# Layer 0's mixing in one block: projection, RWKV, attention and output projection interleaved in one order per engine

## The chip, the cores and the metric

One core of a Trainium2 chip runs the whole program. The metric is the time of one execution in microseconds (us) of device time. Engines are named as the profile names them: PE is TensorE's matmul side and PEld its weight loads, DVE is VectorE, ACT is ScalarE, POOL is GpSimd, SP is SyncE, which here issues all DMAs. All arithmetic is f32.

## The reference, cut to what matters

A decoder trunk of two layers over 256 tokens of width 1024. Each layer has a mixer with a residual add, then a mixture of experts with a residual add. Only layer 0's mixer is touched:

```python
u = rms_norm(h, norm_mix[0])
cols = u @ hyb_w_in[0]                          # 1024 -> 1696 RWKV + 1304 attention columns
y_rwkv = rwkv7_mix(cols[..., :RWKV_COLS], ...)  # 8 heads x 64; recurrence over tokens
y_nsa = nsa_mix(cols[..., RWKV_COLS:], ...)     # 8 query, 2 key heads; 3 branches
h = h + jnp.concatenate([y_rwkv, y_nsa], -1) @ hyb_w_out[0]
```

`rwkv7_mix` shifts its columns by one token, derives decay, gate and learning rate from three low-rank parts, and runs the recurrence `state = state*w + (state@a) b' + v k'`, `y = state@r` for each token, then a norm per head, a bonus term and the gate. `nsa_mix` adds three attentions, each times a gate of its own: over 15 compressed blocks (a two-layer network on 32 tokens each), over selected blocks (with 256 tokens all four blocks are selected, so it is causal attention with its own keys and values), and over a window of 512, again causal here.

## The kernel before, in words

Layer 0's mixer is four blocks, each of which all engines finish before the next begins.

`hyb_in` (lines 270 to 379): x is normed (`norm_act`, `norm_dve`), turned (`turn_pe`, `turn_act`) and projected. The weights come in seven groups of columns through a ring `wr` of three slots; a group's slot is loaded again when TensorE has finished the group three before it. The RWKV columns r, k, v come out channel-major, six jobs of 256 channels (`feat`), the low-rank parts in three small jobs (`lo`), the attention columns token-major in three groups (512, 512 and 280 columns). VectorE applies the token shift.

`rwkv` (from line 381): the recurrence in chunks of 64 tokens. There are 16 slots of 128 rows, each with two chunks of one head in its row halves. First, small products give decay, keys and their norm; then products of 64x64 (`nn`, `bar`, `kar`), masked by VectorE, and turnings (`bt`, `at`, `kt`, `vt`) prepare a triangular system per chunk. It is inverted in five levels (`LEVELS`, line 741 for all its products): in a level TensorE makes `prod` from the level's mask and the inverse so far, ScalarE copies it, TensorE makes two updates (`dT`, `dTT`) and VectorE adds them (line 522) and masks for the next level (line 505). Then come `wu`, the maps and states between chunks (`gains`, `queries`, `step`, `carried`), the part within chunks (`within`), and on VectorE the norm per head, bonus and gate.

`nsa` (from line 899): its weights are loaded, rotary positions applied, then q, keys and the compression's input are turned by head into 64 rows (line 1069). The compression is 64 accumulating matmuls of 64 rows (line 1084). Compressed scores, softmax, turning and output follow (lines 1103 to 1116), then eight units `UNITS` (half of the tokens, branch, key head): `scores` (line 1127; 128 keys for the first half of tokens, 256 for the second), mask and maximum on VectorE (lines 988 to 997), four exponentials on ScalarE (line 1048), turning (line 1139), copy (line 1055), output (line 1146), scaling and sum on VectorE. Unit i+1's scores stand ahead of unit i's turning in TensorE's queue.

`join_hyb` (the function `join`): both halves of `mix` are turned, the output weights loaded, and 32 matmuls (64 instructions, as each f32 matmul is two) give the residual's addend. The router and the experts of layer 0 follow in blocks of their own; their weights are loaded from the start of the router's block on.

The order on each engine is written out by hand in the block's functions, and waits are on per-engine counts: `at(mark)` names a finished operation. A PSUM bank is taken with `take`: the eight banks in turn, waiting for the read of the job that had the bank before.

Of the kernel before, what the change touches and what calls it, by code (L numbers as in the profile page):

```python
# [14 lines left out]
P = 128  # L15
# [56 lines left out]
FEAT, NFEAT = columns([("mu", 12), ("mu_w", 1), ("mu_a", 1), ("mu_g", 1), ("w0", 4), ("a0", 4), ("k_k", 4),  # L72
# [62 lines left out]
def build(nc, a, known, new):  # L135
# [101 lines left out]
    s_ld = {n: sem("ld_" + n) for n in ("small", "gain", "w0", "w1", "w2", "par", "out")}  # L237
# [11 lines left out]
    nsa = sb(hyb, "nsa", [P, HALVES, NSA_COLS])  # L249
    mix = sb(hyb, "mix", [P, HALVES, D])  # L250
    z = sb(hyb, "z", [P, 12, SEQ + 1])
    zlo = sb(hyb, "zlo", [P, 3, SEQ + 1])
    par = sb(hyb, "par", [P, 3 * RW + 2 * RW])
    proj = ExitStack()
    zz, lo3 = sb(hyb, "zz", [P, 12, SEQ]), sb(hyb, "lo3", [P, 3, SEQ])
    gain = sb(proj, "gain", [P, D])
    junk = sb(proj, "junk", [P, D])
    ss = sb(proj, "ss", [P, HALVES])
    rstd = sb(proj, "rstd", [P, HALVES])
    u = sb(proj, "u", [P, HALVES, D])  # L260
    uT = sb(proj, "uT", [P, KD, SEQ])
    wr = sb(proj, "wr", [P, 3, KD, BANK])

    GRP = [(0, 512), (512, 512), (1024, 512), (1536, 160), (1696, 512), (2208, 512), (2720, 280)]

    FJOBS = [(g, j) for g in range(3) for j in range(2)]
    LO = [(0, W_RANK), (W_RANK, A_RANK), (W_RANK + A_RANK, G_RANK)]
    w_hyb = a["hyb_w_in"][0].rearrange("(k p) n -> p k n", p=P)

    with nc.Block(name="hyb_in", no_gpsimd_drain=True) as block:  # L270

        @block.sync
        def _(sp):
            load(sp, "small", h[:, :, :], a["x"][0].rearrange("(t p) d -> p t d", p=P))
            load(sp, "small", cst[:, :], a["tables"])
            load(sp, "small", feat[:, :], a["feat"])
# [922 lines left out]
    hyb.close()  # L1199

# [841 lines left out]
```

## Time and profile before

| | us |
|---|---|
| median of 3 runs | 1801.09 (1800.7 to 1805.3) |
| the profiled execution | 1801.7 |
| its span | 1799.9 |
| TensorE busy | 1611.2 (90%) |
| VectorE, ScalarE busy | 425.4 and 270.6 |
| layer 0's mixer: projection; RWKV; attention; output projection | 0 to 109.8; to 208.3; to 345.9; to 384.9 |

How to read it: a busy TensorE is not TensorE at its peak. Its clock is granted at one of two levels, 2.4 GHz (shown as 1.00) or 1.2 GHz (0.50), and the same matmul lasts about twice as long at the lower one. Idle time of an engine costs nothing unless the work that sets the end waits for it.

### The profile page before, as it was taken

How to read it: one execution, taken by the hardware profiler on the slowest of the kernel's cores; microseconds unless marked ns; L12 is line 12 of the kernel's file. 1: busy time of each engine (PE TensorE's matmuls, PEld its weight loads, DVE VectorE, ACT ScalarE, POOL GpSimd, SP SyncE). 2: the span in 40 equal slices, each digit the busy share in tenths (PEclk: the TensorE clock that was granted, in tenths of full speed). 3: DMA queues.
4: the chain of work that ended last, by engine and by line, in shares of the span. 5: the costliest groups of instructions: out<-in, count | busy, mean ns of one | idle time of the engine just before them, and what ended most of it. 6: DMA issues, size and time to landing. Idle time of an engine off the chain costs nothing. (4 is left out here: it accounts for less than half of the span.)

```text
span 1799.9 us, 21666 instructions
## 1 busy us (share of the span) xinstructions
PE 1611.2 (90%) x8698; PEld 896.2 (50%) x8698; DVE 425.4 (24%) x1053; ACT 270.6 (15%) x525; POOL 8.3 (0%) x12
## 2 busy tenths in 40 slices
PE   6989588877999999999969998968699999999995
PEld 5658486643444343434448746734444434444442
DVE  1138614222111111111115305621311111111111
ACT  2032202221101010101010123211110111110011
POOL 0000000000000000000000001000000000000000
PEclk9979755578999999999979996579799999999998
DMA  6400200248999999999743410042899999999990
GB/s 219 138 1 3 50 0 1 94 162 332 411 411 404 413 405 409 413 404 411 316 153 141 144 71 1 0 187 77 341 415 407 411 404 412 404 412 403 412 393 36
DMA packets 86807, 459.93 MB, mean 256 GB/s; under 512 B 11072, under 2 KB 17344, under 8 KB 37344
## 3 DMA queue, kind: packets, MB, share of 16 engines
q1 hardware_dynamic: 86752, 459.15, 63.8%
q8 instruction: 40, 0.66, 0.2%
q14 instruction: 15, 0.12, 0.0%
HBM read 458.07 MB, written 1.05 MB: 255 GB/s over the span
## 5 line engine op out<-in xcount | busy, mean ns | idle before, releaser
L1513 PE MATMUL bank<-rawffn,xgffn 128*64 128x512 f32 x2048 | 451.9, 594 | 0.0
L1513 PEld LDWEIGHTS bank<-rawffn,xgffn 128*64 128x64 f32 x2048 | 144.2, 137 | 278.0 <-issue 274.1
L1553 PE MATMUL bank<-rawffn,aTffn 128*64 128x512 f32 x1024 | 233.8, 598 | 18.9 <-DVE aTffn L1461 18.9
L1461 DVE TENSOR_TENSOR aTffn<-bank,sgffn 128x256 f32<-128x256 f32 x64 | 27.2, 425 | 659.1 <-ACT sgffn L1433 659.1
L1483 PE MATMUL bank<-selffn,uxffn 128*128 128x128 f32 x1024 | 131.6, 283 | 10.4 <-DVE selwffn L1453 9.1
L1483 PEld LDWEIGHTS bank<-selffn,uxffn 128*128 128x128 f32 x1024 | 122.5, 196 | 35.5 <-issue 24.3
L1553 PEld LDWEIGHTS bank<-rawffn,aTffn 128*64 128x64 f32 x1024 | 67.8, 136 | 140.2 <-issue 109.7
L1522 PE MATMUL bank<-ysffn,selTffn 64*128 64x512 f32 x512 | 127.2, 615 | 1.6 <-DVE ysffn L1471 1.6
L1431 ACT COPY gusffn<-bank 128x512 f32<-128x512 f32 x64 | 37.5, 586 | 560.7 <-PE bank L1513 560.7
L1471 DVE COPY ysffn<-bank 128x512 f32<-128x512 f32 x64 | 44.3, 692 | 194.5 <-PE bank L1553 194.5
L1522 PEld LDWEIGHTS bank<-ysffn,selTffn 64*128 64x128 f32 x512 | 44.1, 186 | 83.8 <-issue 80.5
L1746 PE MATMUL bank<-uT,wr 128*128 128x256 f32 x384 | 85.1, 385 | 0.7 <-ACT uT L232 0.7
L1746 PEld LDWEIGHTS bank<-uT,wr 128*128 128x128 f32 x384 | 74.3, 194 | 11.5 <-ACT uT L232 1.1
L1423 ACT COPY xgffn<-bank 128x512 f32<-128x512 f32 x64 | 37.5, 586 | 225.4 <-PE bank L1483 225.4
L1754 PE MATMUL bank<-wr,uT 128*128 128x512 f32 (+1 forms) x160 | 58.7, 529 | 0.0
L1189 PE MATMUL bank<-wo_ssm,srcT_ssm 128*128 128x512 f32 x128 | 55.2, 593 | 2.5 <-DMA wo_ssm<-in_ssm_w_out 2.5
L1540 PEld LDWEIGHTS bank<-cst,gusffn 128*128 128x128 f32 x256 | 26.8, 141 | 50.1 <-issue 47.0
L362 PE MATMUL bank<-uT,wr 128*128 128x256 f32 x192 | 44.2, 395 | 0.7 <-ACT uT L232 0.7
L1540 PE MATMUL bank<-cst,gusffn 128*128 128x128 f32 x256 | 42.0, 287 | 1.4 <-ACT gusffn L1431 1.4
L1754 PEld LDWEIGHTS bank<-wr,uT 128*128 128x128 f32 x160 | 27.9, 190 | 30.2 <-issue 30.1
L1433 ACT ACTIVATE sgffn<-bank 128x256 f32<-128x256 f32 x64 | 24.6, 384 | 118.4 <-PE bank L1540 118.3
L362 PEld LDWEIGHTS bank<-uT,wr 128*128 128x128 f32 x192 | 38.2, 199 | 6.7 <-ACT uT L232 1.1
(357 smaller groups left out, 1384.5 us busy)
## 6 DMA issues: line engine op xcount, KB each, us to landing
rawffn<-in_moe_w_gate SPq DMA_DIRECT2D x128, 1024.0 KB, 6.7
rawffn<-in_moe_w_up SPq DMA_DIRECT2D x128, 1024.0 KB, 8.8
rawffn<-in_moe_w_down SPq DMA_DIRECT2D x128, 1024.0 KB, 7.4
wr<-in_ssm_w_in SPq DMA_DIRECT2D x10, 2048.0 KB, 9.0
wr<-in_hyb_w_in SPq DMA_DIRECT2D x5, 2048.0 KB, 13.1
wo_ssm<-in_ssm_w_out SPq DMA_DIRECT2D x4, 2048.0 KB, 16.4
wo_hyb<-in_hyb_w_out SPq DMA_DIRECT2D x2, 2048.0 KB, 10.4
cst<-in_tables SPq DMA_DIRECT2D x1, 1208.0 KB, 7.3
```

The lines of the kernel that those rows point to most:

```text
L362: i = nc.tensor.matmul(b[:, c * SEQ:(c + 1) * SEQ], wr[:, g % 3, k, (2 * j + c) * P:(2 * j + c + 1) * P], uT[:, k, :], start=(k == 0), sto ...
L1189: i = nc.tensor.matmul(bs[t][c][:, :], srcT[:, k, t * P:(t + 1) * P], wo[:, k // 4, k % 4, c * BANK:(c + 1) * BANK], start=(k == 0), stop= ...
L1423: nc.scalar.copy(xg[:, :, 4 * half:4 * half + 4, :].rearrange("p x k s -> p k x s"), bank[SIDE_BANK][:, :].rearrange("p (k x s) -> p k x s ...
L1431: nc.scalar.copy(gus[:, :, :], bank[GU_BANK][:, :].rearrange("p (q j) -> p j q", j=4)).then_inc(S["gus"], 1)
L1471: V.tensor_copy(ys[:, :], bank[Y_BANK][:, :]).then_inc(S["y"], 1)
L1483: i = T.matmul(bank[SIDE_BANK][:, k * P:(k + 1) * P].rearrange("p (x s) -> p x s", x=2), ux[:, t, 4 * half + k, :], sel[:, t, :, :], start ...
L1513: i = T.matmul(bank[GU_BANK][CAP * m:CAP * m + CAP, :], xg[:, odd, k, :], raw[:, slot, (k % 4) * FH:(k % 4 + 1) * FH], start=(k == 0), sto ...
L1522: i = T.matmul(bank[ACC[2 * t + n]][:, :], selT[CAP * n:CAP * n + CAP, x, t * P:(t + 1) * P], ys[CAP * n:CAP * n + CAP, :], start=start, s ...
L1540: i = T.transpose(bank[TURN_BANK][:, j * P:(j + 1) * P], gus[:, j, :], C("ident"))
L1553: i = T.matmul(bank[Y_BANK][CAP * n:CAP * n + CAP, :], aT[:, j, :], raw[:, slot, jj * D + n * BANK:jj * D + (n + 1) * BANK], start=(j == 0 ...
L1746: i = nc.tensor.matmul(b[:, c * SEQ:(c + 1) * SEQ], wr2[:, g % 3, k, (2 * j + c) * P:(2 * j + c + 1) * P], uT2[:, k, :], start=(k == 0), s ...
L1754: i = nc.tensor.matmul(b[:, 0:n], uT2[:, k, j * P:(j + 1) * P], wr2[:, g % 3, k, 0:n], start=(k == 0), stop=(k == KD - 1))
```

## The change

The four blocks become one, `hyb`, with one written order per engine. The columns of the input weights are reordered once on the host (attention first, then low-rank, k, r, v), in six groups; the ring has two slots. x is loaded first and ScalarE waits for it alone; the attention weights are loaded behind the first two groups. Attention's pieces stand between the channel-major projection jobs and then between the five levels; units 6 and 7 stand among the steps between chunks. The banks are two pools of four: `left` for projection, attention and join, `right` for RWKV. Head pairs share one 128-row tile: q, keys and the compression's input are turned 128 columns at a time, keys doubled into both row halves, and scores, compressed scores and compression are pairs of 64-row matmuls in rows 0 to 63 and 64 to 127 that go to two banks. Decay and learning-rate columns are one low-rank job. The output projection adds the attention half first, then the RWKV half by halves of tokens; its weights are loaded during the levels and steps. Many tiles now share memory (`front`, `wr`, `z`, `qk`, `zz`), and several VectorE operations no longer wait for the one before.

`by_tokens(g, n)` is the old token-major group (2x8 matmuls of n columns), `by_channels` half of an old channel-major group (16 matmuls of 256 columns), `weights_turned` and `attended` the turning and the output product of a unit, `products` and `grown` the two halves of a level; `masked`, `grown`, `maps`, `carried` and `output` on VectorE hold the operations of before.

```diff
-    turn = {"n": 0, "at": {}, "last": [None] * 8}
-
-    def take(pe, *job):
-
-        b = turn["n"] % 8
-        turn["n"] += 1
+    turn = {"n": {}, "at": {}, "last": [None] * 8}
+
+    def take(pe, *job, pool=tuple(range(8))):
+
+        n = turn["n"].get(pool, 0)
+        turn["n"][pool] = n + 1
+        b = pool[n % len(pool)]
...
@@ the sync queue of the new block
+            load(sp, "x", h[:, :, :], a["x"][0].rearrange("(t p) d -> p t d", p=P))
+            load(sp, "gain", gain, row_src("mix0"))
             load(sp, "small", cst[:, :], a["tables"])
             load(sp, "small", feat[:, :], a["feat"])
-            load(sp, "gain", gain[:, :], row_src("mix0"))
-            for g, (c0, n) in enumerate(GRP):
-                if g >= 3:
-                    sp.wait_ge(*at("group", g - 3))
-                load(sp, f"w{g % 3}", wr[:, g % 3, :, 0:n], w_hyb[:, :, c0:c0 + n])
+            for g in range(2):
+                load(sp, f"w{g}", wr[:, g, :, 0:GRP[g][1]], w_hyb[:, :, GRP[g][0]:GRP[g][0] + GRP[g][1]])
             load(sp, "par", par[0:W_RANK, 0:RW], a["rwkv_w_up"][0])
-            load(sp, "par", par[0:A_RANK, RW:2 * RW], a["rwkv_a_up"][0])
-            load(sp, "par", par[0:G_RANK, 2 * RW:3 * RW], a["rwkv_g_up"][0])
-            load(sp, "par", par[:, 3 * RW:4 * RW], row_src("gn_w"))
-            load(sp, "par", par[:, 4 * RW:5 * RW], row_src("gn_b"))
+            load(sp, "par", par[W_RANK:W_RANK + A_RANK, 0:RW], a["rwkv_a_up"][0])
+            load(sp, "par", par[0:G_RANK, RW:2 * RW], a["rwkv_g_up"][0])
+            load(sp, "par", gn_w, row_src("gn_w"))
+            load(sp, "par", gn_b, row_src("gn_b"))
+            for x, n in enumerate("kv"):
+                load(sp, "nsaw", w2[:, x, :], a["nsa_w2_" + n][0])
+                load(sp, "nsaw", pe_[HD * x:HD * x + HD, :], a["pe_" + n])
+            sp.wait_ge(*at("turn", "mix0", 1, 1))
+            for x, n in enumerate("kv"):
+                load(sp, "nsaw", w1[HD * x:HD * x + HD, :, :], a["nsa_w1_" + n][0].rearrange("(l d) m -> d l m", d=HD))
+            for g in range(2, 6):
+                sp.wait_ge(*at("group", g - 2))
+                load(sp, f"w{g % 2}", wr[:, g % 2, :, 0:GRP[g][1]], w_hyb[:, :, GRP[g][0]:GRP[g][0] + GRP[g][1]])
+            sp.wait_ge(*at("vt", 1))
+            sp.wait_ge(*at("bt", 1))
+            load(sp, "w2", zz[:, :, :].rearrange("p (k c) t -> p k (c t)", k=3), wv_hyb[:, 4:7, :])
+            load(sp, "w2", wo_n[3], wv_hyb[:, 7, :])
+            sp.wait_ge(*at("wu", 1, 1))
+            for k in range(4):
+                load(sp, "wj", wo_r[k], wv_hyb[:, k, :])
...
@@ vector: levels and attention, then the steps
+            scores(2)
+            masked(1)
+            compressed_turned(0)
+            output(1)
+            grown(1)
+
+            scores(3)
+            masked(2)
+            dve.wait_ge(*at("read", "bon"))
+            dve.wait_ge(*at("read", "vt", 1))
+            go(V.tensor_tensor(heads_(pre), heads_(vt), rep(bon[:, :, :].rearrange("p t n -> p (t n)"), HD, 2),
+                               ALU.mult))
+            output(2)
+            compressed_out(0)
+            grown(2)
...
+            scores(7)
+            output(6)
...
+            maps(1)
+            maps(2)
+            maps(3)
+            carried(1)
+            output(7)
+            carried(2)
...
@@ scalar: the same stretch
+            weights_read(1)
+            products_read(1)
+            by_token("vt", vt, 0)
+            by_token("vt", vt, 1)
+            exps(2)
+            weights_read(2)
+            products_read(2)
+            exps(3)
+            by_token("kt", kt, 0)
+            by_token("kt", kt, 1)
+            weights_read(3)
+            products_read(3)
+            exps(4)
...
@@ tensor: projections with pieces between
+            by_tokens(0, 512)
+            new[("group", 0)] = ("pe", PE.n)
+            by_tokens(1, 512)
+            new[("group", 1)] = ("pe", PE.n)
+            by_tokens(2, VG)
...
+            by_channels(3, NK, 0)
+            pe.wait_ge(*at("blk", 1, 1))
+            bs = [take(pe, "hid", "mm", x, pool=left) for x in range(2)]
+            for l in range(CBLK):
+                for x in range(2):
+                    i = T.matmul(bs[x][:, 0:KV * NCMP], w1[HD * x:HD * x + HD, l, :], blk[HD * x:HD * x + HD, l, :],
+                                 start=(l == 0), stop=(l == CBLK - 1))
+                    if l == CBLK - 1:
+                        i.then_inc(pe_done, PE.one(("hid", "mm", x)))
+            by_channels(3, NK, 1)
...
+                bs = [take(pe, "s", i, e, pool=left) for e in range(2)]
+                for m in range(2):
+                    for e in range(2):
+                        o = T.matmul(bs[e][:, m * w:(m + 1) * w], qT[at64(e), 2 * g + m, tok(t)],
+                                     kT[at64(e), br, g, 0:w], start=True, stop=True)
+                        if m:
+                            o.then_inc(pe_done, PE.one(("s", i, e)))
...
+            weights_turned(0)
+            by_channels(5, NV, 0)
+            attended(0)
+            scores(1)
...
@@ tensor: levels 1 and 2
+            weights_turned(1)
+            scores(2)
+            products(1)
+            pe.wait_ge(*at("zz", 11))
+            for t in range(HALVES):
+                turned(("vt", t), [v4[:, c, tok(t)] for c in range(4)], right)
+            compressed_turned(0)
+            attended(1)
+            grown(1)
+            weights_turned(2)
+            scores(3)
+            products(2)
+            compressed_out(0)
+            for t in range(HALVES):
+                turned(("kt", t), [kh[:, c, tok(t)] for c in range(4)], right)
+            attended(2)
+            grown(2)
...
@@ tensor: join
+            js = [[take(pe, "join", "hyb", t, c, pool=left) for c in range(2)] for t in range(HALVES)]
+            pe.wait_ge(*at("read", "turnn", 1))
+            pe.wait_ge(s_ld["w2"], 32)
+            for k in range(4):
+                for t in range(HALVES):
+                    for c in range(2):
+                        T.matmul(js[t][c][:, :], srcn[:, k, tok(t)], wo_n[k][:, c * BANK:(c + 1) * BANK],
+                                 start=(k == 0), stop=False)
+            pe.wait_ge(s_ld["wj"], 64)
+            for t in range(HALVES):
+                pe.wait_ge(*at("mixr", t))
+                turned(("turnr", t), [mixr[:, t, tok(c)] for c in range(4)], right)
+                pe.wait_ge(*at("read", "turnr", t))
+                for c in range(2):
+                    for k in range(4):
+                        i = T.matmul(js[t][c][:, :], srcr[:, k, tok(t)], wo_r[k][:, c * BANK:(c + 1) * BANK],
+                                     start=False, stop=(k == 3))
+                    i.then_inc(pe_done, PE.one(("join", "hyb", t, c)))
...
```

Levels 3 to 5 follow the same pattern: level l has `weights_turned(l)`, `scores(l+1)`, `products(l)`, `attended(l)`, `grown(l)`, and `compressed_turned(1)` with RWKV's `akv` in level 3, `compressed_out(1)` in level 5. Then `weights_turned(6)`, `scores(7)`, `wu`, `attended(6)`, `gains(0)`, `queries(1)`, `gains(1)`, `weights_turned(7)`, `gains(2)`, `queries(2)`, `queries(3)`, `attended(7)`, `within(0)`, the steps, and after the second step the turning of the attention half.

## Rows read from the trace of the kernel before

**Rows 1.** The page: busy time by engine; granted clock in 40 slices of 45 us

```profile
PE 1611.2 (90%) x8698; PEld 896.2 (50%) x8698; DVE 425.4 (24%) x1053; ACT 270.6 (15%) x525; POOL 8.3 (0%) x12
...
PEclk9979755578999999999979996579799999999998
```

**Rows 2.** Windows: length; busy PE, PEld, DVE, ACT, POOL (count); clock; DMA share, GB/s

```profile
0.00:19.19 19.19, 3.65 (x16) 3.27 (x17) 2.86 (x9) 7.70 (x12) 0.20 (x4) 1.00 0.92 339
19.19:63.30 44.11, 44.11 (x193) 38.18 (x193) 8.32 (x15) 2.94 (x5) 0.00 (x0) 1.00 0.35 124
63.30:73.80 10.50, 10.50 (x49) 6.12 (x49) 3.44 (x7) 1.31 (x3) 0.00 (x0) 1.00 0.55 200
73.80:109.80 36.00, 35.22 (x97) 18.07 (x96) 2.74 (x5) 1.93 (x4) 0.00 (x0) 1.00 0.18 56
109.80:150.20 40.40, 31.59 (x276) 22.82 (x276) 28.52 (x34) 19.41 (x32) 0.00 (x0) 0.66 0.01 1
150.20:180.50 30.30, 30.11 (x963) 30.02 (x963) 21.49 (x27) 7.66 (x14) 0.00 (x0) 0.94 0.02 4
180.50:195.90 15.40, 14.59 (x416) 14.31 (x416) 6.61 (x15) 4.37 (x7) 0.00 (x0) 1.00 0.02 4
195.90:208.30 12.40, 0.00 (x0) 0.00 (x0) 11.20 (x21) 0.60 (x2) 0.00 (x0) 0.60 0.00 0
208.30:252.40 44.10, 34.51 (x160) 32.69 (x160) 11.67 (x46) 7.28 (x17) 0.00 (x0) 0.54 0.28 50
252.40:286.00 33.60, 23.24 (x107) 20.50 (x108) 13.22 (x37) 3.25 (x11) 0.00 (x0) 0.50 0.00 0
286.00:345.90 59.90, 52.92 (x192) 43.55 (x192) 22.60 (x48) 19.70 (x68) 0.00 (x0) 0.50 0.00 1
345.90:353.70 7.80, 3.68 (x17) 3.34 (x17) 0.00 (x0) 2.35 (x4) 0.00 (x0) 0.50 0.86 327
353.70:384.90 31.20, 30.18 (x64) 12.96 (x64) 2.77 (x4) 0.00 (x0) 0.00 (x0) 0.92 0.13 53
400.00:900.00 500.00, 477.90 (x2454) 208.83 (x2456) 80.69 (x258) 51.41 (x102) 0.00 (x0) 0.98 0.96 394
```

**Rows 3.** Timeline: ScalarE's first read of x; DMA issues: the load of x

```profile
8.84 0.19 ACT L330 COPY junk<-h 128x1 f32<-128x1 f32 x1 [6.44 <-DMA feat<-in_feat]
...
h<-in_x SPq DMA_DIRECT2D x1, 1024.0 KB, 4.9
```

**Rows 4.** Groups by line and form, TensorE, attention block (208 to 346)

```profile
L1084 PE MATMUL bank<-blk,w 64*128 64x30 f32 x128 | 27.5, 396 | 5.0 <-DVE blk L936 5.0
L1146 PE MATMUL bank<-nsa,pT 128*128 128x64 f32 x96 | 22.6, 426 | 5.4 <-ACT pT L1055 5.4
L1127 PE MATMUL bank<-kT,qT 64*128 64x256 f32 x32 | 15.1, 651 | 0.0
L1139 PE MATMUL bank<-cst,pr 128*128 128x128 f32 x48 | 12.3, 428 | 1.5 <-ACT pr L1048 1.5
...
L1103 PE MATMUL bank<-kcT,qT 64*128 64x15 f32 x32 | 7.0, 371 | 0.3 <-DVE kcT L948 0.3
```

**Rows 5.** Timeline, 141.3 to 144.3: 64x64 products, then 128x128 turnings

```profile
141.37 1.92 PE L720 MATMUL bank<-ar,kh 64*64 64x128 f32 x64
...
143.21 0.86 PEld L678 LDWEIGHTS bank<-cst,bh 128*128 128x128 f32 x8 [0.17 <-issue]
143.22 1.09 PE L678 MATMUL bank<-cst,bh 128*128 128x128 f32 x8
```

**Rows 6.** Groups by form, TensorE, the levels (150.2 to 180.5)

```profile
L741 PE MATMUL bank<-triT,prod 64*64 64x64 f32 x320 | 10.9, 218 | 0.0
```

**Rows 7.** Groups by form, VectorE: levels (two rows), attention block (last row)

```profile
L522 DVE TENSOR_TENSOR triT<-bank,triT 128x512 f32<-128x512 f32 x10 | 6.9, 692 | 4.0 <-PE bank L741 3.5
...
L505 DVE TENSOR_TENSOR lv<-nrb,cst 128x1024 f32<-128x1024 f32 x4 | 4.9, 1222 | 0.1
...
L994 DVE SCALAR_TENSOR_TENSOR pr<-bank,cst 128x512 f32<-128x512 f32 x8 | 5.5, 692 | 8.5 <-PE bank L1127 8.5
```

More of the change, by code:

```diff
@@ new lines, in by_channels @@
+            def by_channels(g, kind, j):
+                w = weights(g)
+                b = take(pe, "feat", kind, j, pool=left)
+                for c in range(2):
+                    for k in range(KD):
+                        i = T.matmul(b[:, c * SEQ:(c + 1) * SEQ], w[:, k, (2 * j + c) * P:(2 * j + c + 1) * P],
+                                     uT[:, k, :], start=(k == 0), stop=(k == KD - 1))
+                i.then_inc(pe_done, PE.one(("feat", kind, j)))
+                if j:
+                    new[("group", g)] = ("pe", PE.n)
@@ new lines, in turned @@
+            def turned(job, cols, pool):
+                b = take(pe, *job, pool=pool)
+                for n, x in enumerate(cols):
+                    i = T.transpose(b[:, n * P:(n + 1) * P], x, ident)
+                i.then_inc(pe_done, PE.one(job))
+            pe.wait_ge(s_ld["small"], 32)
+            turn_pe(pe, "mix0", u, KD, ("u", "mix0"))
+            pe.wait_ge(*at("read", "turn", "mix0", 1, 1))
+            by_tokens(0, 512)
+            new[("group", 0)] = ("pe", PE.n)
+            by_tokens(1, 512)
@@ L652, in _ @@
             pe.wait_ge(*at("kk2"))
-            b = take(pe, "ksum")
+            b = take(pe, "ksum", pool=right)
             for c in range(4):
@@ new lines, in _ @@
+            pe.wait_ge(*at("read", "kT", 1))
+            scores(0)
+            pe.wait_ge(*at("read", "kcT"))
+            bs = [take(pe, "sc", e, pool=left) for e in range(2)]
+            for t in range(HALVES):
+                for m in range(4):
+                    for e in range(2):
+                        i = T.matmul(bs[e][:, (4 * t + m) * NCMP:(4 * t + m + 1) * NCMP], qT[at64(e), m, tok(t)],
+                                     kcT[at64(e), m // 2, :], start=True, stop=True)
+                        if t and m == 3:
+                            i.then_inc(pe_done, PE.one(("sc", e)))
@@ new lines, in _ @@
+            attended(2)
+            grown(2)
+            weights_turned(3)
+            scores(4)
+            products(3)
+            pe.wait_ge(*at("read", "vt", 1))
+            pe.wait_ge(*at("read", "kar", 1, 1))
+            for t in range(HALVES):
+                b = take(pe, "akv", t, pool=right)
+                for e in range(2):
+                    for c in range(4):
+                        for q in range(2):
+                            i = T.matmul(b[at64(q), (4 * e + c) * HD:(4 * e + c + 1) * HD],
+                                         akr[at64(q), slot(t, e, c), 0, :], vt[at64(q), t, head(e, c)],
+                                         start=True, stop=True)
+                i.then_inc(pe_done, PE.one(("akv", t)))
```

1103 lines of the change are left out of this document (548 added, 555 removed).

## The prediction

> **What bounds the kernel now.** I read the page first: TensorE is busy 90% of the span, but the row of its granted clock falls to 5 tenths in slices 6 to 8 [rows 1], which is 225 to 360 us. So a busy share says little there, and the second view is the table of windows, cut at the borders of layer 0's four blocks [rows 2]. Four things are to be seen in it. The projection (19.19 to 109.8) is TensorE back to back at clock 1.00. In the RWKV block, TensorE waits for VectorE ahead of the levels (28.5 us of VectorE in 40.4), runs back to back through them (30.1 of 30.3), and does nothing in the 12.4 us of the head norm. In the attention block (208.3 to 345.9, 137.6 us) TensorE is busy 110.7 us, nearly all at clock 0.50, and idle for 27. The output projection starts 7.8 us after its block, since turning its input and loading its weights lie there alone, and runs 30.2 us. After it the experts run with the DMA engines at share 0.96 (400 to 900): they start behind the block's end and their pace is the DMA's, so whatever layer 0 gains at 384.9 the span gains, one for one. The page's other slices belong to work that the change doesn't touch.
>
> **The change part by part.** All of layer 0's mixing up to the residual now is one block; I add up TensorE's queue in its new order, every piece at the full clock first, and correct for the clock at the end.
>
> *a. Start.* ScalarE's first read of x waited for three loads until 8.84; x alone landed 4.9 us after its issue at 0.74 [rows 3], thus 5.6. The chain behind it keeps its length: the first projection matmul at 19.19−3.2=16.0. The gain row now is the second load; the tables (wanted by TensorE 8 us later than before by ScalarE) hide behind the norm.
>
> *b. Token-major groups and low-rank columns.* The same 512+512+280 columns: 35.2 us [rows 2], by width 82 instructions of 512 columns at 0.43. The three low-rank jobs become two of equal length: 10.5×2/3=7.1. The first window of the projection holds 2.8 us of half clock (44.1 for six jobs of 32 instructions, half as wide and so 0.215 each, 6.9 a job); they stay: 45.1, to 61.1.
>
> *c. Channel-major jobs.* Six at 6.9: 41.4. The ring has two slots for three. A 2 MB load has at least the 13.7 us of a group to land, and takes 6.4 at the 327 GB/s of the join's load [rows 2]; I take no wait. If this cover is gone, 3 us for each of four loads.
>
> *d. Pieces between these jobs.* Attention's prices are those of before [rows 4] halved for the clock, where rows are pairs of 64-row halves halved again. The compression, 128 instructions in 27.5, becomes 13.7 and paired 6.9; the sixteen 128x128 turnings are 0.13 each at full clock [rows 5] against 0.256 at half. In this stretch: turning q and k 2.3, compression 6.9, its second layer 0.7, score units 0 and 1 1.0, compressed scores 1.8 (7.0 before), turned weights and output of unit 0 1.4: 14.1. RWKV's small products lie here too: the 31.6 us of TensorE ahead of the levels, at clock 0.66, are 21 at the full one, and half of them, 10.3, come before the last projection job. One wait stays, 1.5 us for the squared keys (VectorE's shift, then ScalarE) before the norm sum. Together 25.9.
> Does the pairing hold? No row has 64-row operands in both halves with 128 weight columns. The nearest is the level products, 64x64 on two diagonal quarters: 320 in 10.9 us, 34 ns each with the gaps [rows 6], against 214 ns for a 128-column instruction at half clock. I take the full halving; the other end is none, +6.9 for the compression, +5.8 for the scores, +1.8 for compressed scores: +14.
> The Trainium skill (TensorE: Matmul & The Clock Gate, Part 3: Packing small matmuls) says that a weight load runs beside matmuls in flight only where the row group differs, which is what the new row halves offer; by that rule the price is the paired one.
>
> *e. Ahead of the levels.* Here VectorE sets the pace as before, at 0.69 for a 512-wide operation and 1.2 for a 1024-wide one [rows 7]: after the last job come its copy and shift (2.3), four masks of the first product (2.5), three level operations (3.7) and, because the right-hand pool has four banks, four masks of the second product (2.5) among which the turnings wait for their banks: 11.0, and 0.7 for the last turning. 11.7. Sum so far: 61.1+41.4+25.9+11.7=140.1.
>
> *f. Levels.* TensorE's 30.3 us stay. Added: turnings of v and k 1.9, attention units 1 to 5 with the compressed turnings and outputs 18.0 (all 96 output instructions are 22.6 at half clock, 11.3 at full; all 48 turnings 12.3, thus 6.1; all 256-wide scores 15.1, thus 3.8), and 1.6 of handover. 51.8. VectorE in the same stretch has its 21.5 plus attention's 22: 44 of 52 us. It isn't the bound, but nearly: a late unit has 2x0.69 for scores [rows 7], 1.2 for the maximum (1024 wide, as the mask), 1.2 for the level mask, 1.2 for the gate pieces, 1.2 for output, then 4x0.69 for the sums of a level, 10 us against TensorE's 10.4. The first sum of a level is ready some 6.5 us after its start, VectorE comes to it at 8; the tail of the sums then falls behind the next turned weights and scores, which need no sum. So the level lasts 10 to 11 and not 5.7.
>
> *g. Inter-chunk steps.* 15.4 us, plus attention units 6 and 7 on TensorE 6.2, plus VectorE's output(6) ahead of the copies of the level result and output(7) between the two carried states, 3.4: 25.0.
>
> *h. Join.* The attention half of the output projection (32 instructions of 0.43) is 13.7 and covers the 12.4 us of the head norm; its weights were loaded long before. Then the RWKV half 13.7, two turnings with copy 2.6, the last add 1.0: 31.0. The 7.8 us of load and turning go.
>
> Sum: 16.0+45.1+41.4+25.9+11.7+51.8+25.0+31.0=247.9 against 384.9: 137.0 less. Semaphores, marks and table loads change at nothing: ScalarE has 79 us of work in 248 and its loads lie in waits.
>
> Two corrections. *Changing the tile shape*: when 64x64 products give way to 128x128 turnings, the products end at 143.29 by their row, the turnings' first instruction starts at 143.22 [rows 5], and the weight loads beside it stood 0.17 us; nothing bigger is seen. With some 45 such changes now (before about 10) this is between 0 and 8 us; I take 8, since each of them also ends a run of pairs. The Trainium skill (TensorEngine Tiling (Array Packing), Key Properties) says that a change of tiling mode drains the engine. That speaks against this interleaving; by the rule the 8 us are sure, and the trace agrees in size. *Clock*: attention alone never got out of 0.50 though TensorE was busy 88% of its last 60 us [rows 2]; the levels, at 0.94, did. Mixed about one to two, I expect the full clock for most of it, with stretches of half clock at the compression, behind the 3 us wait before the levels, and once or twice in them: 10 us. Ends: 0, and attention's whole 38 us again.
>
> 137−8−10=119. The profiled execution took 1801.7 (span 1799.9, so 1.8 lies around it), 0.6 over the median of the runs, 1801.09: 1801.7−119=1682.7, and I say 1682.
>
> **The rivals.**
> *R1, VectorE in order.* Scores, masks and outputs stand ahead of the level sums in one queue. If their waits (score product, turned weights, output product) fall in series and not beside TensorE's pieces, a level is TensorE's 10.4 plus VectorE's 9: 5x8.6=43 more, 1725. For it: VectorE waits for products at the sums of the levels already [rows 7] and 44 of 52 us leave little slack. Against: the order gives each of its operations a piece of TensorE's that doesn't need it.
> *R2, half clock through the levels.* The mixture counts as attention did. Then levels cost 30 more, attention 38, steps about 10, of which 10 are in the forecast: +68, 1750. For it: 0.50 throughout 208 to 346 with TensorE busy. Against: the levels' mean of 0.94 is 3.6 us at half clock at their start and the full one from there on, and each level has 4.2 us of their products in one run.
> *R3, slower.* Banks were taken from all eight in turn; now a left and a right pool of four, and each take waits for the reader of the fourth before it. There are 149 takes. A handover that is exposed costs the wait and the reader, 0.40+0.69=1.09 us (a sum of a level behind its product [rows 7]). If all are exposed: 149x1.09=162, 25 more than the whole gain of 137: 1827. It decides from 126 exposed takes on; at the few that e counts it is no loss. Against: in the levels at most six banks are in flight and TensorE never stood.
> *R4, the change doesn't do what it says*: the loads of the output weights wait for the turned v and level result, late, or a ring load is late; TensorE waits as in 345.9 to 353.7. Then +8 and 12: 1702.
>
> **How the numbers follow.** Forecast 0.66 (1682, by itself 1660 to 1710: clock and drains 0 to +22, pairing +14, R4 inside), R1 0.18 (1725), R2 0.12 (1750), R3 0.02, no change 0.02. Below, without any correction it is 1665, and e and g may hold 6 us of waits too many: 1659. Above I go past R1's 1725; what is left out is R2 and R3, 0.14, and a few hundredths below. Range 1658 to 1728. A change within 0.3% (5 us, about what this kernel's measurement can tell) needs R3 almost exactly. Faster 0.97, same 0.01, slower 0.02.
>
> **What would show it.** Right: the router's gain load issued near 266 (384.9−119); first projection matmul at 16; the attention half of the join beside the head norm; a level 10 to 12 us with the clock over 0.9; compression about 7 us (14: no pairing). R1: VectorE over 90% busy in the levels, TensorE waiting for level sums. R2: clock near 0.5 in 140 to 190. R3: TensorE waiting for reads of four takes before, everywhere. The forecast is wrong if the block ends after 290 or before 235, or if the stretch of the experts changes its length.

## The result, and the profile after it

The changed kernel takes 1683.38 us (median of 4 runs, 1682.47 to 1685.17) against 1801.24 (4 runs, 1800.7 to 1805.3): ratio 0.9342, 95% interval 0.9326 to 0.9359. The forecast was 1682. The profiled execution took 1682.47, its span is 1680.7. The page's first line and its row of TensorE's granted clock, to be read against [rows 1] (a slice is 42 us now):

```profile
PE 1541.1 (92%) x8670; PEld 838.8 (50%) x8670; DVE 409.9 (24%) x1011; ACT 264.9 (16%) x520; POOL 8.3 (0%) x12
...
PEclk9989977999999999999799955796999999999997
```

The router's gain load, the first thing behind the block, is issued at 267.21 (before: 384.95), so the block is 117.7 us shorter; the span is 119.2 shorter, and the experts behind it run as before. The windows of the changed kernel, cut at the borders of the prediction's steps, with the columns of [rows 2]: start; token-major groups; low-rank jobs and first turnings; channel-major jobs with their pieces; ahead of the levels; levels; level result with unit 6; steps between chunks; join; experts.

```profile
0.00:16.19 16.19, 3.57 (x17) 3.31 (x17) 3.02 (x11) 7.69 (x12) 0.20 (x4) 1.00 0.89 329
16.19:51.28 35.09, 35.09 (x97) 18.27 (x98) 2.19 (x6) 3.29 (x7) 0.00 (x0) 1.00 0.97 248
51.28:60.68 9.40, 9.40 (x53) 6.88 (x52) 3.76 (x8) 2.83 (x7) 0.00 (x0) 1.00 0.06 8
60.68:135.04 74.36, 72.81 (x493) 59.17 (x491) 35.59 (x68) 23.91 (x54) 0.00 (x0) 0.89 0.16 56
135.04:147.67 12.63, 9.85 (x161) 9.22 (x161) 10.04 (x14) 2.52 (x5) 0.00 (x0) 0.75 0.00 1
147.67:200.35 52.68, 52.27 (x1150) 48.58 (x1149) 39.41 (x64) 22.76 (x64) 0.00 (x0) 1.00 0.12 43
200.35:210.05 9.70, 7.73 (x101) 6.91 (x97) 5.88 (x12) 4.22 (x12) 0.00 (x0) 0.98 0.30 94
210.05:235.62 25.57, 24.63 (x384) 23.39 (x384) 7.30 (x20) 5.12 (x9) 0.00 (x0) 0.61 0.13 49
235.62:267.21 31.59, 29.15 (x76) 12.91 (x72) 12.99 (x22) 1.91 (x5) 0.00 (x0) 1.00 0.00 1
281.00:781.00 500.00, 477.90 (x2455) 209.33 (x2456) 80.82 (x263) 52.28 (x102) 0.00 (x0) 0.98 0.97 395
```

Three things are to be seen. The levels, which now carry most of attention, have TensorE busy for 52.27 of 52.68 us at clock 1.00, with VectorE at 39.41. The steps between chunks have TensorE busy 24.63 of 25.57 us too, but at clock 0.61. And the last row answers to the last of [rows 2]: TensorE busy 477.90 us in both, so nothing was given back behind the block.

### The profile page after: what moved, and what is told of

Same layout as the page of the kernel before. It is cut to its first block and busy times, and to the rows that moved or that the text cites. A ratio compares the mean times of both kernels' runs of the same rounds, so it can differ in the third digit from the quotient of the medians.

```text
span 1680.7 us, 21497 instructions
## 1 busy us (share of the span) xinstructions
PE 1541.1 (92%) x8670; PEld 838.8 (50%) x8670; DVE 409.9 (24%) x1011; ACT 264.9 (16%) x520; POOL 8.3 (0%) x12
## 5 line engine op out<-in xcount | busy, mean ns | idle before, releaser
L1650 PE MATMUL bank<-selffn,uxffn 128*128 128x128 f32 x1024 | 131.5, 283 | 10.4 <-DVE selwffn L1620 9.1
```

The source lines that it names most:

```text
L1650: i = T.matmul(bank[SIDE_BANK][:, k * P:(k + 1) * P].rearrange("p (x s) -> p x s", x=2), ux[:, t, 4 * half + k, :], sel[:, t, :, :], start ...
```

## The experiments

Each kernel is the changed one with one edit. "End" is the issue of the router's gain load in the profiled execution, 267.21 in the changed kernel. The span less this end lies between 1409.7 and 1416.4 in all kernels profiled here, so differences of 3 us in an end mean little by themselves. Ratios are to the kernel before, whose median moved between 1797.58 and 1801.24 from one set of runs to the next: to compare an edit with the changed kernel (0.9342, 0.9326 to 0.9359) take the ratios, where 0.001 is 1.8 us. An end is from one execution only.

### VectorE's order in front of the steps

The largest miss was step g. Its place, in the changed kernel, TensorE and then VectorE in the timeline (start, duration, engine, line, operation, tiles, shape, count, idle time ahead and what ended it):

```profile
202.44 3.71 PE L1218 MATMUL bank<-wr,kk 64*64 64x128 f32 x64
206.08 2.00 PE L1038 MATMUL bank<-nsav,pT 128*128 128x64 f32 x16
210.05 0.49 PE L1230 MATMUL bank<-wr,z 64*64 64x64 f32 x4 [1.97 <-DVE wr L654]
210.29 0.46 PE L1232 MATMUL bank<-front 64*64 64x64 f32 x4
```

```profile
208.18 0.42 DVE L442 TENSOR_TENSOR otmp<-bank,den 128x256 f32<-128x256 f32 x1 [2.72 <-PE bank L1038]
208.64 0.42 DVE L445 TENSOR_TENSOR mixn<-mixn,otmp 128x256 f32<-128x256 f32 x1
209.10 1.29 DVE L654 COPY wr<-bank 128x512 f32<-128x512 f32 x2
```

The level result (L1218) is whole at 206.15, but its copies (L654) stand in VectorE's queue behind `output(6)` (L442, L445), which waits for a product that ends at 208.08. TensorE idles 1.97 us, and from there to 231 its clock is low. The edit puts the copies first:

```diff
-            output(6)
             for t in range(HALVES):
                 dve.wait_ge(*at("wu", t, 1))
                 go(V.tensor_copy(wu[:, slot(t, 1, 0):slot(t, 1, 4), :, :], ...), "read", "wu", t, 1)
+            output(6)
```

> Only VectorE's order changes: the two copies of the level result stand ahead of output(6), so TensorE's steps between chunks need not wait 2 us for them. Theory: the fall to half clock at 210 comes from TensorE's idle 2 us, and the steps' own products can't bring it back; then the steps run at clock 1.00, 25.6 us become about 15.5, and with the wait the block ends 11 us earlier (256), the whole near 1672. Rival: the clock falls for the output product of unit 6 in front of the wait, whose instructions wait for weight loads; then clock stays 0.5 in the steps and only the wait goes, -2 us (1681).

Measured: 1670.43 us, ratio 0.9289 (0.926 to 0.9319), end 254.39, thus 12.8 earlier (9.5 by the ratios, whose intervals lie apart). The timeline at the same place, TensorE:

```profile
200.57 3.71 PE L1218 MATMUL bank<-wr,kk 64*64 64x128 f32 x64
204.21 2.00 PE L1038 MATMUL bank<-nsav,pT 128*128 128x64 f32 x16
206.14 0.34 PE L1230 MATMUL bank<-wr,z 64*64 64x64 f32 x4
206.30 0.29 PE L1232 MATMUL bank<-front 64*64 64x64 f32 x4
```

and the window from there to the join:

```profile
206.14:222.81 16.67, 15.66 (x386) 14.78 (x385) 7.73 (x21) 5.13 (x9) 0.00 (x0) 1.00 0.32 119
```

No wait, and the same four products last 0.34 us instead of 0.49. From here to the join are 16.7 us (206.14 to 222.81) instead of 25.6. So of the 12.8 us, 2.0 are the wait, 8.9 are the clock, and 1.9 had come earlier in the block, where nothing was edited: up to 148 us the changed kernel spends 24 us at the low clock and this one 17.

### The wait filled, not removed

Is it the idle time that costs the clock, or VectorE's order in some other way? Here the order stays, and TensorE multiplies a constant into a bank that the next turning overwrites; nobody reads the result.

```diff
             attended(6)
+            filled = take(pe, "ptT", 7, 0, pool=left)
+            for _x in range(2):
+                T.matmul(filled[:, :], ident, cst[:, 0:BANK], start=True, stop=True)
...
-            weights_turned(7)
+            weights_turned(7, filled)        # its first turning goes into that bank
```

> VectorE's order stays, and TensorE runs two matmuls of 512 columns that nobody reads (four instructions, 1.7 us) in the 2 us wait before the steps. Theory (the idle stretch drops the clock): steps at clock 1.00, 9 to 10 us less although the wait stays, near 1674. Rival (the output product of unit 6 in front, or the steps themselves, drop it): steps at 0.5 as now, time unchanged (1683).

Measured: 1673.64 us, ratio 0.9312 (0.929 to 0.9335), end 257.86, thus 9.4 earlier by adding work. By the ratios it is 5.4 and the intervals just overlap, so the window of the steps decides. Timeline, TensorE, and that window:

```profile
205.63 2.00 PE L1043 MATMUL bank<-nsav,pT 128*128 128x64 f32 x16
207.47 1.94 PE L1229 MATMUL bank<-cst 128*128 128x512 f32 x4
209.63 0.34 PE L1238 MATMUL bank<-wr,z 64*64 64x64 f32 x4 [0.23 <-DVE wr L654]
```

```profile
209.63:226.28 16.65, 15.64 (x385) 14.76 (x385) 7.19 (x20) 5.13 (x9) 0.00 (x0) 1.00 0.19 75
```

The steps take 16.65 us, the same as in the kernel before this one. The idle stretch was the cause. The other kernels of this document bear it out. The seven with this wait of 1.97 us (the changed one and those of the sections on the halves of the compression, tile shape, the projection job, banks and the start) all run the steps behind it at the low clock for 17 to 21 us. The five without it run them at 1.00. The Trainium skill (TensorE: Matmul & The Clock Gate, HAM oscillation — how this bites in real kernels) tells of waits for DMA, of 3 to 5 us in its example, that throttle the engine again so that the work behind them starts cold. These runs agree that a wait does it, with 8.9 us lost behind one of only 2.0.

### Attention in one piece ahead of the levels

Does mixing attention with the levels keep the clock up, or does the change gain only by filling waits? The rest of units 1 to 7 stands together ahead of level 1; the same instructions on each engine, in another order.

```diff
@@ tensor
             weights_turned(1)
             scores(2)
+            compressed_turned(0)
+            attended(1)
+            weights_turned(2)
+            scores(3)
...
+            weights_turned(7)
+            attended(7)
             products(1)
...
-            compressed_turned(0)
-            attended(1)
             grown(1)
...
```

> Attention units 1 to 7 with the compressed parts run in one piece ahead of the five levels, on all engines; pairs, pools, join as in the changed kernel. Theory (the mixture with the level products is what keeps attention at the full clock and fills its waits): attention in one piece is at clock 0.5 with its waits, 52 to 57 us; levels 32, steps 15 to 25; together 100 to 114 against 88 now, so 12 to 26 us slower than the changed kernel: 1695 to 1709. Rival (the gain of the attention part is pairing and merged operations, the clock would stay up anyway): TensorE's work is the same, at most +5: 1688.

Measured: 1698.67 us, ratio 0.9433 (0.9403 to 0.9464), end 281.95, thus 14.7 later. Windows (columns as above): attention alone in two parts, then the levels, then the steps and the join:

```profile
154.00:180.00 26.00, 22.37 (x106) 18.05 (x106) 12.51 (x26) 8.73 (x29) 0.00 (x0) 0.54 0.00 0
180.00:204.00 24.00, 21.43 (x157) 19.14 (x155) 9.97 (x20) 7.88 (x23) 0.00 (x0) 0.57 0.01 2
204.00:244.00 40.00, 39.62 (x1219) 39.03 (x1219) 24.74 (x34) 10.27 (x19) 0.00 (x0) 1.00 0.30 104
244.00:282.00 38.00, 33.69 (x191) 16.99 (x185) 15.98 (x30) 4.75 (x9) 0.00 (x0) 1.00 0.02 6
```

Attention by itself runs at the low clock, as before [rows 2], with TensorE waiting 6.2 of its 50 us (for the exponentials and for VectorE); the levels behind it are at 1.00. The steps are too, as VectorE has no `output(6)` to wait for there, which gives back the 10.9 us of wait and clock found above. Net the mixing is worth 15 us (16 by the ratios), and at its own place, with these 10.9, an estimated 25 (14.7+10.9). The clock is the larger part of it: length times missing clock is 22 us in these 50, against 6.2 of waits. The forecast of 12 to 26 us holds, and the rival's +5 does not.

### The compression's two halves one after the other

```diff
-            for l in range(CBLK):
-                for x in range(2):
+            for x in range(2):
+                for l in range(CBLK):
                     i = T.matmul(bs[x][:, 0:KV * NCMP], w1[HD * x:HD * x + HD, l, :], blk[...], ...)
```

> The compression's matmuls are issued all for rows 0 to 63 and then all for rows 64 to 127, no longer in turn; the same 128 instructions. Theory (row halves run side by side): the compression lasts 13.7 us at full clock or more at half, against 9.0, so 5 to 10 us slower: 1688 to 1693. Rival (no overlap of row halves, 9.0 has another cause): no change.

Measured: 1694.95 us, ratio 0.942, end 279.34, thus 12.1 later, more than the 5 to 10 expected. The compression of the changed kernel and then of this one, as windows:

```profile
67.69:76.68 8.99, 8.99 (x130) 8.93 (x129) 1.57 (x3) 0.59 (x1) 0.00 (x0) 0.80 0.01 2
```

```profile
69.75:91.69 21.94, 21.94 (x130) 21.88 (x129) 1.77 (x4) 1.05 (x3) 0.00 (x0) 0.62 0.00 1
```

Length times clock is 7.2 us against 13.6: the pairing halves the compression, and the prediction's two ends (6.9 and 13.8) were both right. It also shortens the stretch that lies at the low clock, which is why the cost is above the one expected: unpaired, the compression lasts 13.0 us longer and not 6.4. The prediction set its paired price beside the Trainium skill (TensorE: Matmul & The Clock Gate, Part 3: Packing small matmuls), by which a weight load runs beside matmuls in flight only where the row group differs. The two times agree with that; the busy shares don't show it, since the weight loads are busy throughout in both windows (8.93 of 8.99 and 21.88 of 21.94).

### More changes of tile shape

The 8 us of the prediction for changes of shape: unit l's output product (128x128) is cut in four and put between the pairs of `prod` (64x64): 6 to 8 changes more in a level, 35 in all.

```diff
                 for s in range(HEADS):
+                    if between is not None and s % 2 == 0:
+                        between(s // 2)          # a quarter of attended(l)
...
-            attended(4)                          # and so for each level
             grown(4)
```

> In each level the output product of the attention unit is cut in four and put between the 64x64 products of the second half of the level's first product: 7 more changes of tile shape per level, 35 in all, no more work. Prediction's term (0.17 us each): 6 us slower, 1689. Rival, by the trace of the changed kernel, where a level with its pieces lasts what the pieces sum to: 0 to +1.

Measured: 1688.29 us, ratio 0.9389 (0.9359 to 0.9418), end 272.44, thus 5.2 later. The levels have low clock in two places here (0.92 in the mean), so only a level at full clock can be compared. Level 4 of the changed kernel, its output product and last `prod`, and the cut one:

```profile
182.56 2.08 PE L1133 MATMUL bank<-amt,wr 64*64 64x64 f32 x64
184.58 2.00 PE L1038 MATMUL bank<-nsav,pT 128*128 128x64 f32 x16
186.50 1.15 PE L1133 MATMUL bank<-kp,kk 64*64 64x64 f32 x32
```

```profile
185.67 1.15 PE L1146 MATMUL bank<-amt,wr 64*64 64x64 f32 x32
186.75 0.66 PE L1035 MATMUL bank<-nsav,pT 128*128 128x64 f32 x4
187.34 0.45 PE L1146 MATMUL bank<-amt,wr 64*64 64x64 f32 x8
187.72 0.66 PE L1035 MATMUL bank<-nsav,pT 128*128 128x64 f32 x4
...
190.52 1.10 PE L1146 MATMUL bank<-kp,kk 64*64 64x64 f32 x32
```

From the first `prod` to the first update are 3.94 us there (182.56 to 186.50) and 4.85 here (185.67 to 190.52). In level 4 there are 2 changes of shape between these points in the changed kernel and 8 in the cut one, so 0.91 for 6 changes, 0.15 us each. Large pieces carry the same price. Start to start, 4 instructions of the output product take 0.59 and 16 take 1.92, thus 0.111 each and 0.15 per piece; 8 of `prod` take 0.38 and 64 take 2.02, thus 0.029 each and again 0.15 per piece. The 45 changes of the change itself are 6.8 us by this, an estimate. They don't stand out as a term of their own, since the old prices were taken over whole pieces with their borders.

### The compression within a projection job

If mixing keeps the clock up, the low stretch at the compression might go as well: two steps of it after each matmul of the job ahead.

```diff
-            by_channels(3, NK, 0)
             pe.wait_ge(*at("blk", 1, 1))
+            for c in range(2):
+                for k in range(KD):
+                    i = T.matmul(kb[:, c * SEQ:(c + 1) * SEQ], w[:, k, c * P:(c + 1) * P], uT[:, k, :], ...)
+                    for l in (2 * (KD * c + k), 2 * (KD * c + k) + 1):     # both halves of steps l
...
```

> The compression's steps are put two by two behind the matmuls of the projection job before it. Theory (9 us of 30-column matmuls in one run drop the clock, which costs 2 us in it and 1.7 in the job behind): clock 1.00 from 60 to 87, 3 to 4 us less. Rival (changing between 64-row and 128-row tiles 32 times costs more than that): same or slower by up to 3.

Measured: 1681.71 us, ratio 0.9341 (0.9313 to 0.9368), end 267.49, no gain by either. Its window over this stretch, and the pieces of it:

```profile
60.00:87.00 27.00, 26.50 (x199) 19.57 (x198) 2.25 (x6) 6.53 (x14) 0.00 (x0) 1.00 0.23 79
```

```profile
61.95 0.63 PE L982 MATMUL bank<-blk,front 64*128 64x30 f32 x8
62.51 0.70 PE L976 MATMUL bank<-uT,wr 128*128 128x256 f32 x2
63.14 0.63 PE L982 MATMUL bank<-blk,front 64*128 64x30 f32 x8
```

The clock is 1.00 throughout, as hoped. But a round of 2 and 8 instructions starts every 1.19 us, 16 rounds are 19.1, while a job (7.07) and the compression at full clock (7.2) are 14.3: 4.8 us lost to 32 changes, 0.15 each. This is the second measure of the price of a change, and it is the same as the first. The clock gives back only 3.4 of it, and a wait of 0.5 us for a copy stands ahead of the first round: the next projection job ends at 87.50, in the changed kernel at 85.32, so at this place the rival holds, 2.2 us slower. Behind it this kernel has no low clock up to 138 us, where the changed one has 10, and then two stretches of it in the levels, where the changed one has none; the sum is nought. The Trainium skill (TensorEngine Tiling (Array Packing), Key Properties) has it that a change of tiling mode drains the engine. Both runs agree that a change costs something; a drain as such is not to be seen in them.

### Banks

Two edits on the pools of PSUM banks. The turnings ahead of the levels take left banks, so that they don't wait for masks of the second product:

```diff
-                turned(("bt", t), [bh[:, c, tok(t)] for c in range(4)], right)
+                turned(("bt", t), [bh[:, c, tok(t)] for c in range(4)], left)
```

(and the same for `at`)

> The four turnings ahead of the levels take their banks from the left pool, which is free there, and need not wait for VectorE's masks of the second product. Theory (the four-bank pool is the cause of TensorE's 1.6 us wait before them): they run right behind the second product; the levels start 2 us earlier, and the clock stays up: -2 to -4 us. Rival: the levels wait for VectorE's masks anyway: under -0.5.

Measured: 1677.94 us, ratio 0.9335 (0.9303 to 0.9367), end 263.24, thus 4.0 earlier. In the timeline of the changed kernel the turnings wait 1.56 us at 144.20 for VectorE; here that wait is gone. By the ratios it is 1.3 us, and the time is not told apart from the changed kernel's.

And one pool for all, as before the change:

```diff
-            left, right = (0, 1, 2, 3), (4, 5, 6, 7)
+            left = right = tuple(range(8))
```

> Both pools become one of eight banks taken in turn, as before the change. Theory (four-bank pools cost little, as only the stretch before the levels waits for banks): within 3 us of the changed kernel, either side, since one queue of banks makes RWKV's takes wait for attention's readers. Rival R3 of the prediction (pools serialise many handovers): 10 us or more faster.

Measured: 1677.63 us, ratio 0.932 (0.9288 to 0.9351), end 263.50, thus 3.7 earlier (4.0 by the ratios, with intervals that overlap): about as much as the turnings alone, and hardly more than the 3 us of the theory. R3 needed them to cost more than the 137 us of the gain.

### The start

```diff
-            load(sp, "gain", gain, row_src("mix0"))      # from behind x
             load(sp, "small", cst[:, :], a["tables"])
             load(sp, "small", feat[:, :], a["feat"])
+            load(sp, "gain", gain, row_src("mix0"))      # to behind feat
...
             act.wait_ge(s_ld["x"], 16)
+            act.wait_ge(s_ld["small"], 32)
```

> ScalarE waits for all three early loads again, and the gain row comes last. Theory of the start: the first projection matmul at 19.2 instead of 16.2, and the end 3.0 to 3.3 us later (270.4), since the token-major groups follow without a gap. Second question, the cold start: before, the first window of the projection held some 2.8 us of half clock, after it none. If that came from the later start, it comes back, and the end is 6 us later (273). If it came from elsewhere, only 3.2.

Measured: 1690.85 us, ratio 0.9374 (0.9353 to 0.9395), end 276.14, thus 8.9 later, more than either number (5.8 by the ratios, with intervals that overlap). The first projection matmul starts at 20.51, 4.3 later, and the 96 instructions of the token-major groups take 35.3 us as in the changed kernel: no slow start. The 4.3 are more than 3.2 because ScalarE's table load (1.28 us) stands at 1.11 in the changed kernel and in that of before, ahead of the loads' arrival, and here at 8.93, behind the waits. The rest is the clock again, in part at the compression and the job behind it:

```profile
56.00:66.00 10.00, 10.00 (x56) 7.38 (x54) 3.77 (x8) 3.61 (x8) 0.00 (x0) 1.00 0.14 35
66.00:88.00 22.00, 22.00 (x168) 19.99 (x167) 1.96 (x5) 4.94 (x10) 0.00 (x0) 0.70 0.22 81
88.00:140.00 52.00, 50.45 (x316) 40.24 (x315) 33.31 (x63) 18.03 (x42) 0.00 (x0) 0.93 0.12 41
```

The changed kernel has 7 us of low clock there (73 to 80) and this one 14 (75 to 89), with the same instructions; some 3 us. In the whole block they have 44 and 55, with two stretches in the levels here. A shift of all work by 4 us moves where the clock falls and comes back.

### The two gains together

The copies first and the turnings in the left pool:

> Both edits together: the copies of the level result ahead of output(6), and the turnings ahead of the levels in the left pool. Adding theory: the two gains are at different places (3 to 4 us ahead of the levels, 12.8 us in the steps), so the block ends 16 us earlier, the gain load is issued near 251.5, and the median is 1667. Rival, the clock: the 4.0 us of the bank edit alone came partly from where half clock fell; then the two do not add, and the end is at 253 to 256, the median 1669 to 1672.

Measured: 1669.45 us (1668.59 to 1675.26), ratio 0.9272 (0.9252 to 0.9292), end 257.69: later than the 251.5 of the adding theory and than the 253 to 256 of the rival. The copies first and one pool of eight:

> The copies ahead of output(6), and one pool of all eight banks. If the order of banks costs only ahead of the levels, this is worth as much as the edit that moves the turnings alone: end near 251 to 252, median 1667. If a wait for the fourth take before hides elsewhere too, it ends earlier than that: below 249. If it is later than 256, the waits in one pool of eight fall on late units of attention instead.

Measured: 1670.05 us (1662.86 to 1672.32), ratio 0.9251 (0.9227 to 0.9275), end 254.06: none of the three cases of the expectation. The three kernels with the copies first (1670.43, 1669.45, 1670.05) are not told apart: the intervals of the first and the last ratio overlap too. All beat the changed one, by 9.5, 12.6 and 16.4 us by the ratios. The second edit does its part in the first of the two: from the last projection job to the levels are 10.4 us (135.77 to 146.13), with the changed kernel's 12.6 beside it. But its levels have a stretch of low clock at their end that the kernel with the copies first alone does not have, while the one with the turnings in the left pool alone has one too (194 to 198):

```profile
188.00:202.00 14.00, 14.00 (x206) 13.02 (x203) 7.92 (x13) 4.33 (x12) 0.00 (x0) 0.76 0.01 2
```

So neither reading is shown. The ends alone don't add, and the ratios would allow it (0.0053 and 0.0007 less apart, 0.0070 together). An estimate takes half of each block's time at the low clock off its end, to leave the work. It gives 245.0 for the changed kernel (44 us low), 245.9 with the copies first (17), 246.1 with the left pool (34) and 245.7 with both (24), but 243.0 and 242.2 for the two with one pool of eight (41 and 24). By it the left pool gives nothing of its own and one pool of eight 2 to 4 us; a gain of that size is smaller than what the clock moves about, and no run here settles it.

## Why the prediction was right, and where it was right by luck

Step by step, forecast and measured, in us:

| step | forecast | measured |
|---|---|---|
| a start | 16.0 | 16.2 |
| b token-major and low-rank | 45.1 | 42.8 (16.19 to 58.94) |
| c, d channel-major jobs and pieces | 67.3 | 76.1 (58.94 to 135.04) |
| e ahead of the levels | 11.7 | 12.6 |
| f levels | 51.8 | 52.7 |
| g steps with units 6 and 7 | 25.0 | 35.3 (200.35 to 235.62) |
| h join | 31.0 | 31.6 |
| changes of shape and clock | 18 | in the rows above |
| end | 266 | 267.2 |

*What held.* Steps a, e, f and h are within 1 us: the loads, VectorE's operations ahead of the levels, the levels' sum of old prices, and the head norm behind the attention half of the join. (e holds 3.2 us of missing clock, in part beside VectorE's work, so its 12.6 for 11.7 owes something to luck.) The pairing was taken at the full halving, which the serial compression confirms for the compression; scores and compressed scores had no run of their own. Attention keeps the full clock in the levels because of the mixing, which attention in one piece confirms. The experts kept their pace, so the block's gain is the span's.

*What failed.* Three terms, which cancelled.
First, the clock: 10 us, at the compression, behind the wait ahead of the levels, and "once or twice" in the levels. Length times missing clock is 8.2 us in the channel-major stretch (74.36 at 0.89, of which 3.4 at the compression and the job behind it), 3.2 ahead of the levels (12.63 at 0.75), none in the levels and 10.0 in the steps (25.57 at 0.61): 21. So two of the three places were right. The third is luck of this kernel: eight of its eleven variants above have one or two stretches of low clock in the levels (3 to 7 us each). The steps, which the forecast left out, are nearly half of it, and their measured cost is 8.9. This is the term that failed most. At full clock g would have been 26.4, near the forecast of 25.0, so its instructions were counted rightly; what was missed is what the wait in it does. The prediction named that wait ("VectorE's output(6) ahead of the copies") and priced it by its length alone.
Second, changes of shape: 8 us. The runs give 0.15 us for each, 6.8 for 45, but not on top of the sum: at full clock no step is longer than its sum of old prices by more than 1.4 us. f is 52.7 for 51.8, and the channel-major stretch, 74.36 at 0.89, is 66.2 at the full clock, for 65.6 forecast (67.3 less the 1.7 of q and k's turning, which lies before it). So most of it must lie in the old prices already, as argued above; no run separates it. In f a part of it is hidden by another error: "TensorE's 30.3 us stay" were taken at clock 0.94 [rows 2], 28.5 at the full one, so f ran 2.7 us over its sum, an estimate.
Third, the 2.8 us of slow start in b, which "stay". They lay in the first job alone, as ScalarE's waits for the first two jobs of the kernel before show (start, duration, operation, idle time ahead), and within it in the first 5 us, as two windows show:

```profile
28.86 0.59 ACT L336 COPY z<-bank 128x512 f32<-128x512 f32 x1 [9.72 <-PE bank L362]
35.77 0.59 ACT L336 COPY z<-bank 128x512 f32<-128x512 f32 x1 [6.32 <-PE bank L362]
```

```profile
19.19:24.20 5.01, 5.01 (x12) 4.03 (x13) 0.00 (x0) 0.00 (x0) 0.00 (x0) 1.00 1.05 388
24.20:28.86 4.66, 4.66 (x23) 4.11 (x22) 0.00 (x0) 0.00 (x0) 0.00 (x0) 1.00 0.42 156
```

The same instructions last 0.42 us each up to 24.20 and 0.20 behind it, the ratio of the two levels. The 1.00 of these rows and of [rows 2] is no reading there: the trace's first record of the granted clock is at 24.20, and the windows count 1.00 ahead of it. So the forecast's reading as half clock fits, and that it would stay was wrong: in the changed kernel the first record is at 15.04, ahead of the first projection matmul at 16.19, and with the late start at 20.38, just ahead of 20.51. Why it comes earlier there is open.
The errors had both signs: 18 us of corrections stood for 21 of clock, less these 2.8, plus some 1 us of the steps' own. The right total owes something to that.

*The rivals.* R1 (VectorE in order) did not come in the levels, but its mechanism is the wait of 1.97 us in front of the steps: one operation in the wrong place of a queue, 2 us of itself and 8.9 by the clock. R2 came in the steps; in the levels it came in none of the variants for more than 7 us at a time. R3 is refuted by one pool of eight, which gives 3.7 us. R4 did not come: the attention half of the join follows the steps without a gap at 235.62, and its two waits for turnings are 0.67 us each.

## What to carry to other kernels

On a TensorE whose clock is granted, price a wait by what it does to the work behind it: 2 us of idle time in front of small matmuls cost 11, and filling it with unread matmuls won back 9. Look in the other engine's queue for an operation that waits, with a ready one behind it that TensorE needs. Interleave starved work with dense work, in pieces of 1 us or more: each change between shapes cost 0.15 us here, whatever the size of the pieces. When a change has moved the time by a tenth, read the terms one by one all the same: here three errors summed to 1 us.

## What the runs showed of the hardware that was not expected

- The low clock outlives its cause. The products of the steps (64x64, 64 columns) keep TensorE busy for all of 20.95 us in the changed kernel and do not lift the clock out of its lower level before 230, while the same products, reached at the full clock, stay at it for 16.7 us. Windows of the changed kernel, the wait and the products behind it:

```profile
208.00:210.05 2.05, 0.08 (x2) 0.04 (x1) 1.80 (x4) 0.00 (x0) 0.00 (x0) 0.89 0.97 372
210.05:231.00 20.95, 20.95 (x293) 20.05 (x295) 3.74 (x11) 2.31 (x5) 0.00 (x0) 0.52 0.15 59
```

- Busy for 100% of a stretch and yet falling: the compression (64 rows, 30 columns) has no idle time at all, and the clock falls within it, 0.80 in 8.99 us paired and 0.62 in 21.94 unpaired.
- Two kernels that differ by one edit at one place show stretches of low clock at other places too (106 to 110 and 195 to 202 with the copies first and the left pool, none of either with the copies first alone). A difference of 3 us between two single profiles of this kernel says nothing.
